# First stage of a two-layer decoder trunk: weights by quarters, and part of a modulation product as four column strips

## The chip, the cores and the metric

One core of a Trainium2 chip runs the whole program. The metric is the device time of one execution in microseconds (us). It is compared between the kernel before and the changed kernel; the median of three runs stands for the kernel before.

## What is computed

Two layers over `x` (1 x 512 x 1024, float32). Only the first mixer's beginning matters here:

```python
c_act = jax.nn.silu(c)
for l in range(DEPTH):
    mod = c_act @ ada_w[l] + ada_b[l]
    sh_m, sc_m, g_m, sh_f, sc_f, g_f = jnp.split(mod, N_MOD, axis=-1)
    h = modulate(rms_norm(x, norm_mix_g[l]), sh_m, sc_m)
    # layer 0: short_conv_mixer
    u = h @ w_in
    b_g, c_g, xv = jnp.split(u, 3, axis=-1)
    ...
```

`modulate` is `h * (1 + scale) + shift`. The first stage of the kernel is therefore: normalise x, compute the 2 x 1024 values `sh_m` and `sc_m` of layer 0 from a 1024 x 2048 piece of `ada_w`, form h, and multiply it with the first 512 columns of the `c_g` third of `sc_w_in`. All later stages (rest of the convolution mixer, MLP, attention, second MLP) are the same in both kernels.

## The kernel before, in words

Everything is kept transposed: a tile of h is 128 features by 512 tokens, and there are 8 of them (index j or k). Each float32 matrix product is made of three faster ones, with every operand split in a high part (rounded copy, on ACT) and a low part (what the rounding left, a subtraction on DVE): high by high, high by low, low by high (`products`, L589 to L592). A block is 128 output features: 8 tiles by three products into one bank of 512 columns. Four blocks form a group with banks 0 to 3 and weight slots 0 to 3.

The order of each engine is written out by hand, and the engines meet at counting semaphores. In the first stage:

- SP issues the loads in one order (L361 to L380): the four row tiles of x, then for each quarter q of the features 8 pieces of `ada_w` (`ada_quarter`, 256 KB each, into one of two buffers `ada_first`), with two weight blocks (`load_block`, 512 KB, rows of 512 bytes) behind each of quarters 0 and 1, and a fifth block (`early_raw`) behind quarter 3. A piece of quarter q waits until the same piece of quarter q-2 was used. Other rows and the next loads follow in the same queue.
- Modulation of a quarter: DVE multiplies pieces by the matching value of `c_act` and adds them up in `ada_acc` (`quarter_steps`, L1619): five pieces of quarter 0 and seven of each other. PE takes the remaining pieces (`quarter_direct`, L712) as products with one column each into bank 6, and adds the sum over the partitions of `ada_acc` (`quarter_sum`, L724). DVE adds the bias and makes the gain (`quarter_gain`, L1632).
- h tiles: ACT squares the rows of x (`token_square`, with the small Exp for silu behind the first of four, L1156 to L1160) and scales two of them, DVE the other two, into `x_unit`; PE transposes two tiles of a quarter into banks 4 and 5 (`unit_pair`, L700); ACT makes `tc` or `ta` and the high part (`first_tile`, L1169), DVE the low part (`first_low`, L1641).
- PE also transposes x itself for the residual stream (`x_turn`, L733; ACT copies it out, `x_tile`), and multiplies (`open_block`, L745). A block there waits for its whole weight block and its split. L754 to L788 write the order out.

Behind the stage PE transposes a few more rows (L791) and goes on with blocks 4 to 7 (L792 to L795), block 4 from its own early copy.

Of the kernel before, what the change touches and what calls it, by code (L numbers as in the profile page):

```python
# [54 lines left out]
ADA_STEPS = [(0, 1, 2, 3, 4)] + 3 * [tuple(range(KT - 1))]  # L55
ADA_DIRECT = [tuple(k for k in range(KT) if k not in steps) for steps in ADA_STEPS]
STEP_NO = {(q, k): n for n, (q, k) in enumerate((q, k) for q in range(QUARTERS) for k in ADA_STEPS[q])}
DIRECT_NO = {(q, k): n for n, (q, k) in enumerate((q, k) for q in range(QUARTERS) for k in ADA_DIRECT[q])}

# [35 lines left out]
def yoco_trunk(nc, x_in, c_in, ada_w, ada_b, norm_mix_g, norm_mlp_g, sc_w_in, sc_conv, sc_w_out,  # L95
# [23 lines left out]
    def stacked(offset, specs):  # L119
        made = []  # L120
        for name, shape, dt in specs:
# [31 lines left out]
    early_lo, = stacked(region_kv + size([P, KT, T + CONV - 1], F32) + size([P, NMOD * D], F32)  # L153
                        + size([P, TT, D], F32), [("early_lo", [P, KT, P], F32R)])
# [10 lines left out]
    raw, = stacked(region_w, [("raw", [P, GROUP, KT, P], F32)])  # L165
    rms = new("rms", [P, T], F32)
# [4 lines left out]
    early_hi, = stacked(region_qk + size([P, 2, T], F32), [("early_hi", [P, KT, P], F32R)])  # L171
# [3 lines left out]
    early_raw, = stacked(region_tb, [("early_raw", [P, KT, P], F32)])  # L175
# [3 lines left out]
    tv = new("tv", [P, T], F32)  # L179
# [40 lines left out]
    with ExitStack() as ctx:  # L220
# [23 lines left out]
        ada_direct = sem("ada_direct")  # L244
# [104 lines left out]
        def _(sp):  # L349
# [14 lines left out]
            def ada_quarter(q):  # L364

                for k in range(KT):
                    if (q - 2, k) in STEP_NO:
                        sp.wait_ge(ada_stepped, STEP_NO[q - 2, k] + 1)
                    elif q >= 2:
                        sp.wait_ge(ada_direct, DIRECT_NO[q - 2, k] + 1)  # L370
# [60 lines left out]
            for s in range(1, GROUP):  # L431
                sp.wait_ge(pe_done, s + 1)
# [153 lines left out]
        def _(pe):  # L586
# [16 lines left out]
            def dense(g, jj, hi, lo, ready=None, between=None, weights=None):  # L603
# [9 lines left out]
                elif weights:  # L613
                    last = part_of(b, 0, out, hi, lo, range(KT), ready, weights=weights)
# [85 lines left out]
            def unit_pair(q):  # L700

                for i in range(2):
                    j = 2 * q + i
                    if q:
                        pe.wait_ge(hs_ok, j - 1)
# [6 lines left out]
            def quarter_direct(q):  # L712
# [3 lines left out]
                for k in ADA_DIRECT[q]:  # L716
                    pe.wait_ge(ada_in[q % 2][k], 16 * (q // 2 + 1))
                    for n in range(4):
                        one = mm(bank[6][:, n:n + 1], ada_first[:, q % 2, k, n // 2, n % 2 * P:(n % 2 + 1) * P],
                                 c_act[:, k:k + 1], start=(k == ADA_DIRECT[q][0] and n == 0), stop=False,  # L720
                                 skip_group_check=True)
                    one.then_inc(ada_direct, 1)

            def quarter_sum(q):  # L724

                pe.wait_ge(ada_stepped, STEP_NO[q, ADA_STEPS[q][-1]] + 1)
                for n in range(4):
                    c = n // 2 * KT + 2 * q + n % 2
                    one = mm(bank[6][:, n:n + 1], ada_acc[:, c * P:(c + 1) * P], ones[:, 0:1], start=False,
# [15 lines left out]
            def open_block(b, tiles):  # L745

                last = part_of(b, b, bank[b], h_hi, h_lo, tiles, lambda k: pe.wait_ge(h_ok, H_MIX0 + k + 1))
                if tiles[-1] == KT - 1:
                    last.then_inc(pe_done, 1)
# [1292 lines left out]
```

## Time and profile before

| what | value |
|---|---|
| median of 3 runs | 1212.68 us (1211.74 to 1213.3) |
| the profiled execution | 1214.36 us |
| its span in the profile | 1211.7 us |
| granted TensorE clock, mean | 0.992 of full |
| PE busy | 1186.0 us, 98% of the span |
| DVE, ACT busy | 767.4 us (63%), 502.2 us (41%) |
| chain that ended last | PE 85%, DVE 7%, ACT 3%, issue 2% |

The span lies between the first and the last instruction; the execution's own time has 2.7 us around it. Busy time of PE says that something was in the array, not that it ran at its peak: the end of a matmul is modelled, and the clock can be granted at half. The chain is followed back from the last instruction to what released each step.

### The profile page before, as it was taken

To read this page: it belongs to the slowest core of one execution; us is meant where nothing else is said; L and a number is where in the kernel's file an instruction comes from. 1 tells how busy PE (TensorE), PEld (TensorE's weight loads), DVE (VectorE), ACT (ScalarE), POOL (GpSimd) and SP (SyncE) were. 2 spreads that over 40 slices of the span, in tenths; PEclk is the share of its full clock that TensorE was granted. 3 is DMA by queue.
4 is the path that set the end of the run, shared out by engine and by line. 5 is a ranking of instruction groups with operands and counts; after the bars stand their busy time and mean duration, and the time that the engine had idled before them with its cause. 6 is when DMAs were issued, how large, how long until landed. Compare 5 with 4: busy or idle time off the path is not lost.

```text
span 1211.7 us, 17089 instructions
## 1 busy us (share of the span) xinstructions
PE 1186.0 (98%) x5891; PEld 1000.2 (83%) x5891; DVE 767.4 (63%) x1117; ACT 502.2 (41%) x818; POOL 24.8 (2%) x37
## 2 busy tenths in 40 slices
PE   6999999999999999999999999999999999999998
PEld 5788888888888888888968888888888888888886
DVE  5557788876565575565888889886843443443441
ACT  5422332542331232332677777864631332331421
POOL 2000000000000000002020000000000000000000
PEclk7899999999999999999999999999999999999999
DMA  9487564466666665332345554451333333323333
GB/s 318 154 247 226 186 207 141 140 209 208 179 187 199 197 197 167 104 88 72 87 105 141 134 128 105 122 140 29 95 104 89 102 100 91 104 87 104 92 100 87
DMA packets 231697, 168.75 MB, mean 139 GB/s; under 512 B 5620, under 2 KB 214684, under 8 KB 231644
## 3 DMA queue, kind: packets, MB, share of 16 engines
q1 hardware_dynamic: 231452, 167.92, 47.8%
q8 instruction: 33, 0.54, 0.2%
q14 instruction: 20, 0.16, 0.0%
q0 software_dynamic: 32, 0.07, 0.0%
q10 hardware_dynamic: 160, 0.06, 0.0%
HBM read 153.24 MB, written 2.10 MB: 128 GB/s over the span
## 4 chain that ended last, share of the span: by engine, by line
PE 85%; DVE 7%; ACT 3%; issue 2%; DVEq 0%; ACTq 0%
PE bank L590 26%; PE bank L592 26%; PE bank L591 26%; PE bank L937 2%; PE bank L919 1%; PE bank L909 1%; PE bank L910 1%; DVE ta L1536 1%; DVE w_lo L1496 1%; DVE tc L1536 1%; ACT w_hi L1078 1%; PE bank L690 1%; DVE ada_acc L1719 0%; DVE h_lo L1545 0%; DVE h_lo L1543 0%
## 5 line engine op out<-in xcount | busy, mean ns | idle before, releaser
L590 PE MATMUL bank<-h_hi,w_hi 128*128 128x512 f32 (+1 forms) x888 | 338.3, 381 | 4.2 <-DVE w_lo L1496 1.7
L591 PE MATMUL bank<-h_lo,w_hi 128*128 128x512 f32 (+1 forms) x888 | 333.9, 376 | 0.0
L592 PE MATMUL bank<-h_hi,w_lo 128*128 128x512 f32 (+1 forms) x888 | 333.7, 376 | 0.0
L1078 ACT ACTIVATE w_hi<-raw 128x1024 fp32r<-128x1024 f32 x187 | 196.6, 1055 | 267.6 <-DMA raw<-in_mlp_w 221.2
L590 PE MATMUL bank<-g_hi,w_hi 128*128 128x512 f32 (+1 forms) x688 | 260.4, 379 | 0.0
L1496 DVE TENSOR_TENSOR w_lo<-raw,w_hi 128x1024 fp32r<-128x1024 f32 x187 | 227.9, 1221 | 47.7 <-ACT w_hi L1078 45.0
L592 PE MATMUL bank<-g_hi,w_lo 128*128 128x512 f32 (+1 forms) x688 | 257.8, 375 | 0.0
L591 PE MATMUL bank<-g_lo,w_hi 128*128 128x512 f32 (+1 forms) x688 | 257.6, 374 | 0.0
L590 PEld LDWEIGHTS bank<-h_hi,w_hi 128*128 128x128 f32 x888 | 168.2, 189 | 37.6 <-issue 6.8
L592 PEld LDWEIGHTS bank<-h_hi,w_lo 128*128 128x128 f32 x888 | 168.3, 190 | 30.1
L591 PEld LDWEIGHTS bank<-h_lo,w_hi 128*128 128x128 f32 x888 | 168.4, 190 | 29.4 <-issue 0.5
L592 PEld LDWEIGHTS bank<-g_hi,w_lo 128*128 128x128 f32 x688 | 129.5, 188 | 23.4
L591 PEld LDWEIGHTS bank<-g_lo,w_hi 128*128 128x128 f32 x688 | 129.6, 188 | 23.2 <-issue 0.5
L590 PEld LDWEIGHTS bank<-g_hi,w_hi 128*128 128x128 f32 x688 | 129.6, 188 | 22.9 <-issue 0.5
L1764 DVE SCALAR_TENSOR_TENSOR x<-bank,mod,x 128x512 f32 (+1 forms) x63 | 47.2, 750 | 141.1 <-PE bank L592 139.7
L1816 DVE TENSOR_TENSOR tb<-ta 128x512 f32<-128x512 f32 x64 | 44.3, 692 | 128.5 <-ACT ta L1276 128.5
L1276 ACT ACTIVATE ta<-bank 128x512 f32<-128x512 f32 x64 | 38.2, 597 | 197.7 <-PE bank L592 197.7
L1719 DVE SCALAR_TENSOR_TENSOR ada_acc<-ada_raw,c_act,ada_acc 128x1024 f32 (+1 forms) x80 | 102.2, 1277 | 2.3 <-DMA ada_raw<-in_ada_w 1.7
L1820 DVE TENSOR_TENSOR g_lo<-tb,g_hi 128x512 f32 (+1 forms) x64 | 44.3, 693 | 15.0 <-ACT g_hi L1278 12.5
L1278 ACT ACTIVATE g_hi<-ta 128x512 f32 x64 | 40.5, 633 | 8.1
L1381 ACT ACTIVATE probs<-bank,neg_max 128x512 f32<-128x512 f32 (+1 forms) x64 | 33.0, 526 | 26.2 <-DVE neg_max L1915 25.3
L1099 ACT ACTIVATE tb<-x 128x512 f32<-128x512 f32 x15 | 9.5, 632 | 55.4 <-DVE x L1764 49.7
(208 smaller groups left out, 1041.0 us busy)
## 6 DMA issues: line engine op xcount, KB each, us to landing
raw<-in_mlp_w SPq DMA_DIRECT2D x128, 512.0 KB, 4.1
ada_raw<-in_ada_w SPq DMA_DIRECT2D x40, 1024.0 KB, 5.7
raw<-in_sc_w_in SPq DMA_DIRECT2D x23, 512.0 KB, 5.9
ada_first<-in_ada_w SPq DMA_DIRECT2D x32, 256.0 KB, 7.1
raw<-in_w_kv SPq DMA_DIRECT2D x16, 512.0 KB, 4.0
raw<-in_sc_w_out SPq DMA_DIRECT2D x8, 512.0 KB, 4.4
raw<-in_q_w SPq DMA_DIRECT2D x8, 512.0 KB, 4.8
keys<-qk SPq DMA_DIRECT2D x16, 256.0 KB, 3.1
```

Source lines behind the costliest of these rows:

```text
L590: mm(out[:, cols], weights_hi, hi[:, k, cols], start=(k == 0), stop=False)
L591: mm(out[:, cols], weights_hi, lo[:, k, cols], start=False, stop=False)
L592: return mm(out[:, cols], weights_lo, hi[:, k, cols], start=False, stop=(k == KT - 1))
L1078: go(w_hi[:, jj, :, :], raw[:, jj, :, :], ACT.Copy).then_inc(hi_ok, 1)
L1276: go(ta[:, jj % 2, :], bank[jj][:], ACT.Relu).then_inc(bank_free, 1)
L1278: go(tile3(g_hi, j), ta[:, jj % 2, :], ACT.Square).then_inc(g_hi_ok, 1)
L1381: go(probs[:, P_OFF[qt]:P_OFF[qt] + n], bank[at_bank][:, c0:c0 + n], ACT.Exp, bias=neg_max[:, s:s + 1], accum_out=p_sum[:, s:s + 1]).then_ ...
L1496: tt(w_lo[:, jj, :, :], raw[:, jj, :, :], w_hi[:, jj, :, :], ALU.subtract).then_inc(lo_ok, 1)
L1719: stt(out=acc, in0=ada_raw[:, s, half * D:(half + 1) * D], scalar=col(c_act, k), in1=acc, op0=ALU.mult, op1=ALU.add).then_inc(ada_used, 1)
L1764: stt(out=tile3(x, j), in0=bank[jj][:], scalar=mcol(layer, part, j), in1=tile3(x, j), op0=ALU.mult, op1=ALU.add).then_inc(bank_free, 1)
L1816: tt(tb[:, s, :], ta[:, s, :], ta[:, s, :], ALU.mult).then_inc(g_a, 1)
L1820: tt(tile3(g_lo, j), tb[:, s, :], tile3(g_hi, j), ALU.subtract).then_inc(g_ok, 1)
```

## The change

The four column blocks of the first group are no longer loaded and split one by one. Their weights come as four quarters of rows (tiles 2q and 2q+1 for all 512 columns, 512 KB, rows of 2 KB), one behind each quarter of `ada_w`, and each quarter is split by one ACT and one DVE instruction of 1024 columns. PE takes the products tile by tile for all four blocks. Of each quarter's 8 pieces DVE steps the first four. PE takes the other four as float32 products of 512 columns: the stationary operand `c_wide[:, k, :]` is 32 columns wide (column 0 is `c_act`, the rest zero), and the output of strip i is partitions 32i to 32i+31 of bank 6. DVE then adds bank 6 to `ada_acc` (`quarter_add`). The odd h tile of each pair is scaled and shifted by DVE, no longer by ACT. The fifth block has no copy of its own: it is loaded into slot 0 once tiles 0 and 1 are used. ACT makes the small Exp behind all four squares.

```diff
@@ SP
             for q in range(QUARTERS):
                 ada_quarter(q)
-                if q < 2:
-                    load_block(2 * q, c_g(2 * q))
-                    load_block(2 * q + 1, c_g(2 * q + 1))
-            sp.wait_ge(hi_ok, 1)
-            sp.dma_start(early_raw[:], c_g(GROUP)).then_inc(raw_in[0], 16)
+                sp.dma_start(first_raw[:, 2 * q:2 * q + 2, :],
+                             sc_w_in[0].rearrange("(k p) n -> p k n", p=P)[:, 2 * q:2 * q + 2, D:D + GROUP * P]
+                             ).then_inc(raw_in[q], 16)
+            sp.wait_ge(first_used, 1)
+            load_block(0, c_g(GROUP))
...
@@ PE
-            def quarter_direct(q):
+            def quarter_strips(q):
 
                 if q:
                     pe.wait_ge(ada_red, q)
-                for k in ADA_DIRECT[q]:
+                for i in range(STRIPS):
+                    k = STRIPS + i
                     pe.wait_ge(ada_in[q % 2][k], 16 * (q // 2 + 1))
-                    for n in range(4):
-                        one = mm(bank[6][:, n:n + 1], ada_first[:, q % 2, k, n // 2, n % 2 * P:(n % 2 + 1) * P],
-                                 c_act[:, k:k + 1], start=(k == ADA_DIRECT[q][0] and n == 0), stop=False,
-                                 skip_group_check=True)
-                    one.then_inc(ada_direct, 1)
+                    mm(bank[6][32 * i:32 * i + 32, :], c_wide[:, k, :], ada_first[:, q % 2, k, :, :], start=True, stop=True,
+                       skip_group_check=True).then_inc(ada_strip, 1)
...
+            def first_products(k, blocks=range(GROUP)):
+
+                pe.wait_ge(lo_ok, k // 2 + 1)
+                pe.wait_ge(h_ok, H_MIX0 + k + 1)
+                for b in blocks:
+                    if k == 0:
+                        pe.wait_ge(x_ok, b + 1)
+                    w_cols = slice(b * P, (b + 1) * P)
+                    last = products(bank[b], first_hi[:, k, w_cols], first_lo[:, k, w_cols], h_hi, h_lo, k)
...
+            unit_pair(0)
+            pe.wait_ge(c_ok, 2)
+            quarter_strips(0)
+            x_turn(4)
             quarter_sum(0)
+            unit_pair(1)
+            quarter_strips(1)
+            first_products(0, range(0, 2))
+            quarter_sum(1)
+            first_products(0, range(2, GROUP))
+            first_products(1)
+            unit_pair(2)
+            quarter_strips(2)
...
@@ ACT
-            token_square(0)
+            for t in range(TT):
+                token_square(t)
             act.wait_ge(cols_ok, 1)
             go(c_tmp[:], cols[:, R_C:R_C + KT], ACT.Exp, scale=-1.0).then_inc(silu_e, 1)
-            for t in range(1, TT):
-                token_square(t)
...
@@ DVE
+            def quarter_add(q):
...
+                dve.wait_ge(ada_stepped, (q + 1) * STRIPS)
+                dve.wait_ge(ada_strip, (q + 1) * STRIPS)
+                tt(acc, bank[6][:].rearrange("p (a c) -> p a c", a=2), acc, ALU.add).then_inc(ada_added, 1)
+
+            def odd_tile(q):
...
+                ts(hs_slot(j, ALL), bank[5][:], gains[:, 0, j:j + 1], mcol(0, 0, j), ALU.mult,
+                   ALU.add).then_inc(odd_ok, 1)
```

Where instructions move. On PE, from the first transposes of x to the first products; names are output<-inputs, `ada_first` holds the pieces of `ada_w`, `x_unit` the normalised rows. Before:

```order
L742 MATMUL bank<-ident,x_rows 128x128 x20
L719 MATMUL bank<-c_act,ada_first 128x1 x12
L709 MATMUL bank<-ident,x_unit 128x128 x8
L729 MATMUL bank<-ones,ada_acc 128x1 x4
L742 MATMUL bank<-ident,x_rows 128x128 x4
L590 MATMUL bank<-h_hi,w_hi 128x512
```

and with the change:

```order
L741 MATMUL bank<-ident,x_rows 128x128 x16
L710 MATMUL bank<-ident,x_unit 128x128 x8
L720 MATMUL bank<-ada_first,c_wide 32x512 x4
L741 MATMUL bank<-ident,x_rows 128x128 x4
L728 MATMUL bank<-ones,ada_acc 128x1 x4
L710 MATMUL bank<-ident,x_unit 128x128 x8
L720 MATMUL bank<-ada_first,c_wide 32x512 x4
L592 MATMUL bank<-h_hi,first_hi 128x512
```

The second pair of transposes and the second quarter's strips now stand ahead of the first product; they stood behind it.

On DVE, quarter 0's sums and its gain, up to the first low part of h (`w_lo`, `first_lo` are the weight's low part). Before:

```order
L1671 TENSOR_SCALAR x_unit<-x_rows,tok 128x1024
L1629 SCALAR_TENSOR_TENSOR ada_acc<-ada_first,c_act,ada_acc 128x2x256 [waits ada_stepped,ada_in02]
L1629 SCALAR_TENSOR_TENSOR ada_acc<-ada_first,c_act,ada_acc 128x2x256 [waits ada_stepped,ada_in03]
L1629 SCALAR_TENSOR_TENSOR ada_acc<-ada_first,c_act,ada_acc 128x2x256 [waits ada_stepped,ada_in04]
L1496 TENSOR_TENSOR w_lo<-raw,w_hi 128x1024 [waits hi_ok]
L1636 TENSOR_TENSOR mod<-bank,ada_bias 128x2x2 [waits ada_turned]
L1615 SCALAR_TENSOR_TENSOR gains<-mod,cols 128x2 [waits ada_red]
```

and with the change:

```order
L1626 SCALAR_TENSOR_TENSOR ada_acc<-ada_first,c_act,ada_acc 128x2x256 [waits ada_stepped,ada_in03]
L1634 TENSOR_TENSOR ada_acc<-bank,ada_acc 128x2x256 [waits ada_strip,ada_stepped]
L1648 TENSOR_TENSOR first_lo<-first_raw,first_hi 128x1024 [waits hi_ok]
L1655 TENSOR_TENSOR mod<-bank,ada_bias 128x2x2 [waits ada_turned]
L1612 SCALAR_TENSOR_TENSOR gains<-mod,cols 128x2 [waits ada_red]
L1642 TENSOR_SCALAR tc<-bank,gains,mod 128x512 [waits unit_turned,mod_ok]
```

An addition that waits for all four strips stands ahead of the split and the gain, and one more h tile behind them.

## Rows read from the trace of the kernel before

**Rows 1.** By stretch: length; busy PE, PEld, DVE, ACT, POOL; granted clock, DMA, GB/s
```profile
0.00:22.50 22.50, 11.34 (x66) 10.61 (x66) 9.99 (x23) 14.02 (x24) 6.53 (x17) 0.90 1.00 317
22.50:62.60 40.10, 38.81 (x177) 32.70 (x178) 23.50 (x36) 15.79 (x23) 1.82 (x1) 0.80 0.63 188
62.60:110.00 47.40, 47.40 (x210) 38.92 (x209) 29.18 (x31) 13.40 (x15) 0.00 (x0) 1.00 0.81 247
```

**Rows 2.** Timeline: PE's first product, its idle time, and the stage's end
```profile
22.56 0.76 PE L590 MATMUL bank<-h_hi,w_hi 128*128 128x512 f32 x1 [1.04 <-DVE h_lo L1543]
...
40.15 1.05 PE L729 MATMUL bank<-ones,ada_acc 128*128 128x1 f32 x8 [1.22 <-DVE ada_acc L1629]
...
62.57 0.23 PE L791 MATMUL bank<-ident,rows_a 74*128 74x74 f32 x1
```

**Rows 3.** Chain that ended last: start, length, what; PE's pieces of the stage
```profile
42.48 0.43 PE bank L591
...
47.04 0.44 PE bank L742 x4
...
51.62 0.87 PE bank L709 x8
52.49 0.79 PE bank L719 x8
53.28 0.89 PE bank L729 x8
...
55.20 0.23 PE bank L591
```

**Rows 4.** Busy time by stretch again: granted clock where it is half, and before it rises
```profile
18.00:34.90 16.90, 14.57 (x53) 12.40 (x53) 13.36 (x22) 10.31 (x17) 0.00 (x0) 0.50 1.12 336
...
41.90:45.00 3.10, 3.10 (x9) 2.45 (x8) 2.33 (x4) 2.51 (x4) 0.00 (x0) 0.50 0.02 6
...
30.20:34.90 4.70, 4.70 (x14) 3.82 (x15) 3.60 (x8) 3.92 (x6) 0.00 (x0) 0.50 1.10 348
```

**Rows 5.** Groups of instructions up to 63 us: busy us, mean ns of one
```profile
L1629 DVE SCALAR_TENSOR_TENSOR ada_acc<-ada_first,c_act,ada_acc 128x512 f32<-128x512 f32 x22 | 16.5, 749 | 2.1 <-DVE ada_acc L1629 0.5 <-DMA ada_first<-in_ada_w 0.5
...
L1496 DVE TENSOR_TENSOR w_lo<-raw,w_hi 128x1024 fp32r<-128x1024 f32 x4 | 4.9, 1225 | 1.8 <-ACT w_hi L1078 1.8
...
L1078 ACT ACTIVATE w_hi<-raw 128x1024 fp32r<-128x1024 f32 x4 | 4.2, 1048 | 1.6 <-DMA raw<-in_sc_w_in 1.6
...
L1175 ACT ACTIVATE tc<-bank,mod,gains 128x512 f32<-128x512 f32 x4 | 3.1, 778 | 5.6 <-issue 5.6
...
L1543 DVE TENSOR_TENSOR h_lo<-tc,h_hi 128x512 fp32r<-128x512 f32 x4 | 2.8, 692 | 1.6 <-ACT h_hi L1178 1.6
```

**Rows 6.** Timeline of SP and ACT in the front, and issue to landing of x's loads
```profile
0.75 1.84 SPq L362 DMA_DIRECT2D x_rows<-in_x  x4
...
8.29 0.21 ACT L1158 ACTIVATE c_tmp<-cols 128x8 f32<-128x8 f32 x1 [2.58 <-DVE cols L1650]
...
13.07 2.19 ACT L1167 ACTIVATE x_unit<-x_rows,tok 128x1024 f32<-128x1024 f32 x2 [0.83 <-DVE tok L1667]
...
DMA to landing us min/median/max: 3.8/5.3/6.8
```

**Rows 7.** Rates of transfer (columns as in rows 1), and a wait for quarter 2's first piece
```profile
15.00:16.00 1.00, 1.00 (x11) 1.00 (x11) 0.89 (x2) 0.26 (x1) 0.00 (x0) 1.00 1.20 290
...
21.00:22.00 1.00, 0.52 (x3) 0.12 (x1) 0.28 (x1) 0.97 (x3) 0.00 (x0) 0.50 1.10 348
...
29.04 0.49 DVE L1626 TENSOR_SCALAR ada_acc<-ada_first,c_act 128x512 f32<-128x512 f32 x1 [0.60 <-DMA ada_first<-in_ada_w]
```

**Rows 8.** Float32 products of 256 columns (min/median/max ns), and split ones of 256 columns
```profile
L631 PE MATMUL bank<-ssum,ones x12: 377/380/484, 213.6 to 853.3; 128*128 128x256 f32 x12
...
848.90 0.28 PE L590 MATMUL bank<-o_hi,out_hi 128*128 128x256 f32 x1
849.02 0.28 PE L591 MATMUL bank<-o_lo,out_hi 128*128 128x256 f32 x1
```

More of the change, by code:

```diff
@@ L52 @@
 X_BANK = [0, 1, 2, 3, 7, 7, 7, 7]
[L55 to L58, printed above, removed]
+STRIPS = 4
 KVQ_ORDER = [("k", 0), ("v", 0), ("k", 1), ("q", 0), ("q", 1), ("v", 1)]
@@ L601, in part_of, with dense @@
                 return last
-            def dense(g, jj, hi, lo, ready=None, between=None, weights=None):
+            def dense(g, jj, hi, lo, ready=None, between=None):
                 if not isinstance(g, int) or g > 0:
@@ L612, in dense @@
                     last = part_of(b, s, out, hi, lo, range(6, KT), ready)
-                elif weights:
-                    last = part_of(b, 0, out, hi, lo, range(KT), ready, weights=weights)
                 else:
@@ L743, in x_turn @@
                 v.then_inc(x_turned, 1)
[L745 to L749, printed above, removed]
+            def first_products(k, blocks=range(GROUP)):
[6 more added lines that the diff above has]
+                    last = products(bank[b], first_hi[:, k, w_cols], first_lo[:, k, w_cols], h_hi, h_lo, k)
+                    if k == KT - 1:
+                        last.then_inc(pe_done, 1)
+                if b == GROUP - 1 and k % 2 and k < KT - 1:
+                    last.then_inc(first_used, 1)
@@ L780, in _ @@
-            quarter_direct(3)
-            quarter_sum(3)
-            open_block(2, Q[2])
-            open_block(3, Q[2])
-            for tile in Q[3]:
-                for b in range(2):
-                    open_block(b, range(tile, tile + 1))
-            open_block(2, Q[3])
-            open_block(3, Q[3])
+            unit_pair(1)
[4 more added lines that the diff above has]
+            first_products(1)
@@ new lines, in _ @@
+            unit_pair(2)
+            quarter_strips(2)
+            first_products(2, range(0, 2))
+            quarter_sum(2)
+            first_products(2, range(2, GROUP))
+            first_products(3)
+            unit_pair(3)
+            quarter_strips(3)
+            first_products(4, range(0, 2))
+            quarter_sum(3)
+            first_products(4, range(2, GROUP))
+            x_turn(5)
+            first_products(5)
+            x_turn(6)
+            first_products(6)
+            x_turn(7)
@@ L789, in _ @@
+            first_products(7)
             pe.wait_ge(rows_more, 16 * 8)
@@ L791, in _ @@
             turn(bank[7][:, 0:ROWS], rows_a[:], ident[0:ROWS, 0:ROWS]).then_inc(cols_pe, 1)
-            dense(1, 0, h_hi, h_lo, weights=(early_hi[:].rearrange("p (s k) c -> p s k c", s=1),
-                                             early_lo[:].rearrange("p (s k) c -> p s k c", s=1)))
-            for jj in range(1, GROUP):
+            for jj in range(GROUP):
                 dense(1, jj, h_hi, h_lo)
@@ L1183, in x_tile @@
                 go(x[:, j, :], bank[X_BANK[j]][:], ACT.Copy).then_inc(x_ok, 1)
[L1185 to L1195 removed]
+            for j in range(4):
+                x_tile(j)
+            split_first(0)
+            first_pair(0)
+            x_tile(4)
+            split_first(1)
+            first_pair(1)
+            split_first(2)
+            first_pair(2)
+            split_first(3)
             x_tile(5)
[L1197 to L1199 removed]
+            first_pair(3)
             x_tile(6)
[L1201 to L1203 removed]
+            split(1, 0)
             x_tile(7)
[L1205 to L1207 removed]
             act.wait_ge(unit_rest_ok, TT - 2)
@@ L1617, in gain, with quarter_steps @@
                 dve.wait_ge(mod_ok, count)
-            def quarter_steps(q, first, last):
+            def quarter_steps(q, first=0, last=STRIPS):
                 acc = ada_acc[:, 0:2 * D].rearrange("p (a q c) -> p a q c", a=2, q=QUARTERS)[:, :, q, :]
-                for k in ADA_STEPS[q][first:last]:
+                for k in range(first, last):
                     dve.wait_ge(ada_in[q % 2][k], 16 * (q // 2 + 1))
```

150 lines of the change are left out of this document (70 added, 80 removed).

## The prediction

> **What bounds the kernel.** I read the busy time by stretch first. From 62.6 us on PE is busy 47.40 of 47.40 us at full clock [rows 1], so whatever the first stage gains or loses is carried to the end unchanged. Only the end of that stage matters: the transpose at 62.57 us that closes it [rows 2]. In the front, up to 22.5 us, PE is half idle and waits for data and gains; from the first product at 22.56 us it is busy 38.81 of 40.10 us, but at a mean clock of 0.80 [rows 1, 2].
>
> Those 40.0 us can be taken apart with the pieces of the chain at full clock [rows 3]: 96 products by 0.228 us are 21.9; three pairs of h tiles transposed, by 0.87, are 2.6; three times the direct products of one piece, by 0.79, 2.4; three sums, by 0.89, 2.7; two transposes of x, by 0.44, 0.9. One wait of 1.2 us for DVE's last sum [rows 2] makes 31.7. The rest is clock: it is at half (1.2 GHz) from 18.0 to 34.9 us and from 41.9 to 45.0 us [rows 4], where a product takes 0.43 instead of 0.23 us [rows 3]. Of this 12.4 and 3.1 us lie behind the first product; half of it, 7.8 us, is lost. That explains 39.5 of 40.0 us; I keep the 0.5 us as what such a sum misses.
>
> **The change, part by part.**
>
> *Front.* ACT sat idle for 2.58 us before the small Exp, with three row tiles of x still to be squared behind it [rows 6]. x's fourth tile, the last of four issues from 0.75 to 2.59 us, so issued at about 2.2 us, and 6.8 us under way at the longest [rows 6], lands at 9.0. Without the wait its square ends near 10.3 instead of 11.6 us, so that the last scaled rows are ready at about 14.1 instead of 15.26 us (13.07 + 2.19) [rows 6]: 1.2 us earlier. PE's first four transposes of x and the Exp itself are hidden in front of that.
>
> *Loads.* Pieces of `ada_w` land every 0.75 us (256 KB at 348 GB/s), column blocks at 290 GB/s [rows 7]. Quarter 2's first piece landed at 29.04 us [rows 7]. Backwards from there, less its 0.75, four column blocks by 1.81 and quarter 1's eight pieces by 0.75, quarter 0's last piece landed at 15.1 us. It still does, and then 512 KB (1.5 us at 348 GB/s) instead of 1 MB (3.6 us) lie ahead of quarter 1: its last piece lands at 22.6 us, quarter 2's at 30.1, quarter 3's at 37.7. SP issues some 7 us ahead of the landing, and its new waits (for DVE's steps, for the strips of the quarter before last) are met before that. I cost the loads at nothing; the cover is PE's queue, which reaches quarters 2 and 3 at 35 and 44 us. Block 4's load now stands behind quarter 3 and the first two tiles' products, at about 34 us; it is wanted at 58 us. The rows and later loads queued behind it on SP are not needed before that either.
>
> *DVE and ACT.* DVE steps 16 pieces instead of 26: minus 10 by 0.75 us; plus four additions and four odd tiles, which I take at the 0.69 us of another pass over 512 columns [rows 5]; an addition reads a PSUM bank, so it can't be cheaper. The splits are 1.05 us on ACT and 1.23 us on DVE [rows 5], four as before plus the fifth. A quarter costs DVE 4 steps 2.7, addition 0.7, gain 0.4, odd tile 0.7, split 1.2 and two low parts 1.4: 7.1 us. PE needs 9.3 us for one (below), so I cost DVE at nothing behind the first gain; the wait of 1.2 us goes.
>
> *Strips.* They take the place of the direct products, four per quarter. The trace has no strip. A full float32 product of 256 columns shows two records of 0.38 us, where a split product of 256 columns shows one of 0.28 and its successor starts 0.12 us later [rows 8]; so each float32 record holds the array for 0.12 + 0.10 = 0.22 us, and a product of 512 columns takes two records by 0.43: 0.855 us. Four strips thus cost between 0.86 us (all at once) and 3.42 us (one behind the other). The nearest row is the full product's, two records in order on the same columns of the array. I take what follows when records are kept in order but those of different column strips may overlap: the second record of a strip runs beside the first of the next, five times 0.43, 2.14 us a quarter.
>
> The Trainium skill speaks on both sides of this. "TensorE: Matmul & The Clock Gate" (Part 3) says that products in different column groups run concurrently, with a measured 2.38 times for three column strips, and a span of one product plus some 4 ns per further strip; by that the strips would be the 0.86 us, and the sum 56.2. The same section says that weight loads overlap with running products only where the row group differs, which would put these strips, all on the same rows, one behind the other: the 3.42 us. This trace shows weight loads under products of the same rows (32.70 us of loads within 40.10 us in which PE is hardly idle [rows 1]), so it does not bear that rule out for full arrays; strips no row shows.
>
> *Chain to the start of the dense part.* Rows ready 14.1; pair transposed 15.0; strips 17.2; addition 17.9; split on DVE to 19.1; meanwhile sum to 18.9; gain 19.6; ACT's even tile (0.78 [rows 5]) 20.4. There PE takes the second pair, and from there on it always has work.
>
> *From there.* 96 products 21.9; three pairs 2.6; three quarters of strips 6.4; three sums 2.7; three transposes of x 1.3: 34.9 us. Clock: the two rises of before came 4.7 and 3.8 us after dense work had begun (30.2 to 34.9, and 41.2, behind the sum, to 45.0) [rows 2, 4]. Quarter 1's strips begin at about 22.3 us and end at 26.6 at half clock. If float32 strips count as dense the rise comes near 26.6, if not near 31; I take 28.5, so half speed from 20.4 to 28.5 loses 4.05 us. The fall at 41.9 had behind it 4 us of small products, transposes and a wait; that stretch is gone. With the 0.5 us: 20.4 + 34.9 + 4.05 + 0.5 = **59.9 us** against 62.57, minus 2.7 us.
>
> The profiled execution stands 1.7 us above the median (1214.36 against 1212.68). I put the difference on the median: **1210.0 us**. The bound below and above which a measurement of this kernel can tell a change from none is about 0.2%, 2.4 us: below 1210.3, above 1215.1.
>
> **Rivals.**
>
> A. *Strips all at once* (0.86 us). The quarter's addition ends at 16.6, but the split waits for its high part (16.6 + 1.05) and the even tile is out at 20.1; then 31.1 us of work, 0.6 of wait for quarter 1's last piece, 3.9 lost to the clock, 0.5: 56.2, which is 6.4 us less: 1206.3. For it: outputs lie on separate partitions. Against: two records per product, in order.
>
> B. *Strips one behind the other* (3.42 us), the slower side. Place: PE's queue, between a pair's transposes and the six products. The even tile comes at 21.7; 38.8 us of work, 4.05, 0.5: 65.0, or 2.5 us more: 1215.2. Each microsecond per quarter costs four, so this rival decides from 2.8 us per quarter on. For it: the only float32 rows. Then the change does not do what its strips are for, though weights, sums and clock still gain.
>
> C. *The clock stays at half longer.* Forecast as above, but the rise waits until 35 us, as it did before [rows 4], or a second fall comes: half of 6.5 us more, 63.1, 0.6 us slower: 1213.3. The six products between strips and sum speak against it.
>
> **How the numbers follow.** Forecast 50%, A 17%, B 25%, C 8%. The forecast's own range, with the clock's rise between 26.6 and 31 us and 1 us for the front, is 1208.2 to 1212.3; just over half of it is under 1210.3. Faster: 28 of the 50 and A's 17, and 2 of C: 47%. Within 0.2%: 22 of the 50, 6 of B (its centre is on the bound, but a late rise is more likely than an early one there), 5 of C: 33%. Slower: 19 of B, 1 of C: 20%. The range reaches from A, 1206.0, to B with a late rise, 1216.0.
>
> **What would show it.** The stage's closing transpose at 59 to 61 us. Records of strips: starts 0.43 us apart at full clock with strips overlapping, against all four within 0.9 us (A) or eight by 0.43 (B). The second pair at 20 to 21 us; no wait of PE for DVE from there on; one spell of half clock, ending at 27 to 31 us; PE gapless behind the stage. It would be wrong if PE waited for additions or low parts in every quarter, or if loads of the last quarters landed behind 45 us.

## The result, and the profile after

| | before | changed |
|---|---|---|
| median of the runs compared | 1212.99 us (4 runs) | 1205.43 us (4 runs, 1204.52 to 1205.57) |
| ratio | | 0.9925, 95% interval 0.9908 to 0.9941 |
| span in the profile | 1211.7 us | 1203.5 us |
| closing transpose of the stage | 62.57 us [rows 2] | 54.38 us |

The change is faster by 7.6 us, where 2.7 were forecast and 1206.0 was the lower end of the range. The closing transpose moved by 8.2 us and the span by 8.2: all of it lies in the first stage. The second run of the same kernel (below) closed at 54.18.

Busy time by stretch of the changed kernel (columns as in rows 1): the front, from the first product to the closing transpose, 47.4 us behind it, and the spell at half clock:

```profile
0.00:24.00 24.00, 12.95 (x62) 7.77 (x62) 12.78 (x28) 14.51 (x24) 6.53 (x17) 0.93 0.99 330
24.00:54.40 30.40, 30.40 (x166) 24.01 (x166) 18.76 (x31) 12.88 (x20) 1.82 (x1) 1.00 0.87 278
54.40:101.80 47.40, 47.32 (x210) 38.93 (x209) 29.34 (x31) 13.13 (x16) 0.00 (x0) 1.00 0.69 210
20.80:23.80 3.00, 3.00 (x9) 0.55 (x8) 2.90 (x5) 0.73 (x3) 0.00 (x0) 0.50 1.08 365
```

From the first product on PE is busy without a gap and at full clock (products start 0.23 us apart): 30.4 us, where rows 1 have 40.1 us at 0.80. The first product itself comes later than before, at 24.0 instead of 22.56 us, because a pair and the strips of quarter 1 now stand ahead of it.

PE's timeline in the changed kernel, without its products with h (start, length, what, and the idle time before it with its releaser):

```profile
14.63 1.26 PE L720 MATMUL bank<-ada_first,c_wide 128*32 128x512 f32 x8
15.82 0.66 PE L741 MATMUL bank<-ident,x_rows 128*128 128x128 f32 x4
16.87 1.05 PE L728 MATMUL bank<-ones,ada_acc 128*128 128x1 f32 x8 [0.40 <-DVE ada_acc L1634]
19.75 1.24 PE L710 MATMUL bank<-ident,x_unit 128*128 128x128 f32 x8 [1.83 <-ACT tc L1178]
20.92 3.18 PE L720 MATMUL bank<-ada_first,c_wide 128*32 128x512 f32 x8
25.52 0.95 PE L728 MATMUL bank<-ones,ada_acc 128*128 128x1 f32 x8
30.55 1.03 PE L710 MATMUL bank<-ident,x_unit 128*128 128x128 f32 x8
31.52 1.06 PE L720 MATMUL bank<-ada_first,c_wide 128*32 128x512 f32 x8
...
40.01 1.06 PE L720 MATMUL bank<-ada_first,c_wide 128*32 128x512 f32 x8
...
54.38 0.23 PE L791 MATMUL bank<-ident,rows_a 74*128 74x74 f32 x1
```

A float32 product of 512 columns leaves two records in the trace. Four strips, eight records, take 1.06 us, and only 1.0 us passes until the next instruction starts. The strips' own records in quarter 2, by stretch (length; busy PE, PEld; clock, DMA, GB/s), show them side by side:

```profile
31.50:31.70 0.20, 0.18 (x4) 0.16 (x8) 1.00 1.08 348
31.70:31.90 0.20, 0.20 (x4) 0.00 (x0) 1.00 1.07 338
31.90:32.50 0.60, 0.60 (x8) 0.00 (x0) 1.00 1.11 352
```

Four records are under way before 31.9 us. I read them as one per strip, since records on the same columns start 0.43 us apart (e1 below). All eight weight loads lie within 0.16 us, and they go on while these products already run. From 31.9 us on the second records join.

No sum after the first waits for DVE. The strips of quarter 1 take 3.18 us: the timeline of their weight loads shows 0.93 us of waits for pieces, the last of which landed at 22.22 us, and the clock was at half.

```profile
21.49 0.18 PEld L720 LDWEIGHTS bank<-ada_first,c_wide 128*32 128x32 f32 x2 [0.38 <-DMA ada_first<-in_ada_w]
22.22 0.18 PEld L720 LDWEIGHTS bank<-ada_first,c_wide 128*32 128x32 f32 x2 [0.55 <-DMA ada_first<-in_ada_w]
```

The chain that ended last, at the front (start, length, piece). It runs through the first quarter of the weight, not through x:

```profile
8.34 7.82 DMA first_raw<-in_sc_w_in
16.16 0.02 issue
16.18 1.06 ACT first_hi L1169
17.25 0.02 issue
17.27 1.23 DVE first_lo L1648
...
18.60 0.17 DVE gains L1612
```

DVE's timeline around quarter 1's sum shows that DVE now waits for PE, for the strips and for the sum:

```profile
24.21 0.69 DVE L1634 TENSOR_TENSOR ada_acc<-bank,ada_acc 128x512 f32<-128x512 f32 x1 [0.40 <-PE bank L720]
26.50 0.16 DVE L1655 TENSOR_TENSOR mod<-bank,ada_bias 128x4 f32<-128x4 f32 x1 [1.60 <-PE bank L728]
```

### The profile page after: what moved, and what is told of

The parts are those of the page before. It is cut to its first block, busy times and chain, and to the rows that moved or that the text cites. A ratio compares the mean times of both kernels' runs of the same rounds, so it can differ in the third digit from the quotient of the medians.

```text
span 1203.5 us, 17044 instructions
## 1 busy us (share of the span) xinstructions
PE 1179.1 (98%) x5875; PEld 989.4 (82%) x5875; DVE 765.7 (64%) x1118; ACT 499.3 (41%) x814; POOL 24.8 (2%) x37
## 4 chain that ended last, share of the span: by engine, by line
PE 85%; DVE 7%; ACT 3%; issue 2%; DMA 1%; SPq 1%; DVEq 0%; ACTq 0%
PE bank L592 26%; PE bank L594 26%; PE bank L593 26%; PE bank L935 2%; PE bank L917 1%; PE bank L907 1%; PE bank L908 1%; DVE ta L1533 1%; DVE w_lo L1493 1%; DMA first_raw<-in_sc_w_in 1%; DVE x L1788 1%; DVE tc L1533 1%; ACT w_hi L1076 1%; PE bank L690 1%; DVE ada_acc L1743 1%
## 5 line engine op out<-in xcount | busy, mean ns | idle before, releaser
L592 PE MATMUL bank<-h_hi,w_hi 128*128 128x512 f32 (+1 forms) x864 | 326.8, 378 | 3.2 <-DVE w_lo L1493 1.7
L594 PE MATMUL bank<-h_hi,w_lo 128*128 128x512 f32 (+1 forms) x864 | 323.2, 374 | 0.0
L593 PE MATMUL bank<-h_lo,w_hi 128*128 128x512 f32 (+1 forms) x864 | 323.1, 374 | 0.0
L1076 ACT ACTIVATE w_hi<-raw 128x1024 fp32r<-128x1024 f32 x184 | 193.4, 1054 | 257.9 <-DMA raw<-in_mlp_w 220.7
L1493 DVE TENSOR_TENSOR w_lo<-raw,w_hi 128x1024 fp32r<-128x1024 f32 x184 | 224.4, 1222 | 47.5 <-ACT w_hi L1076 44.7
L592 PEld LDWEIGHTS bank<-h_hi,w_hi 128*128 128x128 f32 x864 | 162.8, 188 | 34.2 <-issue 5.1
L594 PEld LDWEIGHTS bank<-h_hi,w_lo 128*128 128x128 f32 x864 | 162.8, 188 | 28.9
L593 PEld LDWEIGHTS bank<-h_lo,w_hi 128*128 128x128 f32 x864 | 162.9, 189 | 28.3 <-issue 0.5
L592 PEld LDWEIGHTS bank<-g_hi,w_hi 128*128 128x128 f32 x688 | 129.7, 189 | 22.7 <-issue 0.5
L1378 ACT ACTIVATE probs<-bank,neg_max 128x512 f32<-128x512 f32 (+1 forms) x64 | 33.0, 526 | 26.2 <-DVE neg_max L1939 25.3
```

The lines of the kernel that those rows point to most:

```text
L592: mm(out[:, cols], weights_hi, hi[:, k, cols], start=(k == 0), stop=False)
L593: mm(out[:, cols], weights_hi, lo[:, k, cols], start=False, stop=False)
L594: return mm(out[:, cols], weights_lo, hi[:, k, cols], start=False, stop=(k == KT - 1))
L1076: go(w_hi[:, jj, :, :], raw[:, jj, :, :], ACT.Copy).then_inc(hi_ok, 1)
L1378: go(probs[:, P_OFF[qt]:P_OFF[qt] + n], bank[at_bank][:, c0:c0 + n], ACT.Exp, bias=neg_max[:, s:s + 1], accum_out=p_sum[:, s:s + 1]).then_ ...
L1493: tt(w_lo[:, jj, :, :], raw[:, jj, :, :], w_hi[:, jj, :, :], ALU.subtract).then_inc(lo_ok, 1)
```

## The experiments

Two theories stood at the start. Theory 1: the four strips run side by side in the array; they are cheap, and with them the work is short. Theory 2: strips are not cheap, and the gain is clock, or the weights' new order. The runs also separate the change into its halves. Where nothing else is said, an experiment is an edit of the changed kernel, and its median is compared with runs of the kernel before on the same chip. Timelines and closing transposes come from the one profiled execution. In some runs it stood above the median: by 2.1 us in e2, 1.3 in e4, 1.0 in e8, 3.0 in e11, and 1.7 in the kernel before.

### e1: all strips on the same columns

```diff
-                    mm(bank[6][32 * i:32 * i + 32, :], c_wide[:, k, :], ..., start=True, stop=True,
+                    mm(bank[6][0:32, :], c_wide[:, k, :], ..., start=(i == 0), stop=(i == STRIPS - 1),
```

DVE adds 32 partitions instead of 128. A column group is what one strip takes, 32 of the array's 128 columns. 

> All four strips of a quarter are put on the same 32 columns of the array and accumulate there; only those 32 partitions are added. Theory 1 (the changed kernel's strips are cheap, 1.0 us for four, because they sit in different column groups and run beside each other): here four take 4 x 0.855 = 3.4 us at full clock. That is 2.4 us more in quarters 2 and 3 each, 2 to 4 in quarter 1 and 1 to 2 in quarter 0: the stage's closing transpose near 63 us instead of 54.4, the run 1213 to 1215 us. Theory 2 (a product with a stationary operand of 32 columns streams faster wherever it sits): four still take about 1 us and the run stays at 1205 to 1206 us.

Measured: 1214.28 us, ratio 1.0003 (0.9992 to 1.0015); closing transpose at 62.17 us. PE's timeline of that run, one row of the four:

```profile
34.22 3.62 PE L720 MATMUL bank<-ada_first,c_wide 128*32 128x512 f32 x8
```

The next instruction starts 3.55 us later. The same eight records on four column groups took 1.0 us. That is 2.55 us each in quarters 2 and 3. The second pair stands at 22.20 us, 2.45 later than in the changed kernel, and quarter 1's strips add only 0.4 us, since in the changed kernel they waited for pieces and ran at half clock. Without the overlap the whole change is worth nothing, although this run shows full clock in every stretch from 15 to 63 us. Theory 1 is right about the strips.

### e2: one-column products for the same four pieces

The strips are replaced by 16 products with one column, as the kernel before made them for its one or three pieces, and the addition goes. 

> The same four pieces per quarter as 16 one-column products in place of the strips, no addition on DVE. By queue time alone (16 by 0.2 us = 3.2 us instead of 1.0) quarters 1 to 3 cost 2.2 us more each and quarter 0 about 1: 1212 to 1213 us. Theory 3 (what also shortened the spell at half clock, 3.4 us in the changed kernel against 15.5 us behind the first product before, is that PE streams wide products where it had one-column ones): the clock falls again here, as early as 18 us, and is half for 10 us or more, so 3 to 5 us on top: 1215 to 1218 us. If the clock had nothing to do with it, one spell of 3 to 4 us stays.

Measured: 1228.49 us, ratio 1.0115 (1.009 to 1.014); closing transpose at 79.65 us. PE's timeline shows one quarter at half and one at full clock, and the stretches from 16 to 42 us and 50 to 55 us show why the time is so far above what was expected:

```profile
27.41 6.83 PE L721 MATMUL bank<-c_act,ada_first 128*128 128x1 f32 x32
...
45.58 3.63 PE L721 MATMUL bank<-c_act,ada_first 128*128 128x1 f32 x32
```

```profile
16.00:26.00 10.00, 8.61 (x42) 8.55 (x42) 3.52 (x8) 2.85 (x5) 0.00 (x0) 0.50 1.10 353
26.00:38.00 12.00, 12.00 (x53) 11.42 (x51) 3.44 (x6) 2.17 (x4) 0.00 (x0) 0.50 0.83 267
...
50.00:55.00 5.00, 5.00 (x18) 4.23 (x17) 2.04 (x4) 1.63 (x3) 0.00 (x0) 0.50 0.00 2
```

PE is busy 12.00 of 12.00 us from 26 to 38 us, with one-column products, then with products of 512 columns and a sum, and still has half clock. One-column products cost 3.6 us a quarter at full clock, and the clock was at half behind each lot of them: until 42 us behind the first two, and from 49.6 to 56.3 and 63.4 to 69.8 us behind the others. Its Theory 3 named the right direction and less than half of the size.

### e3 and e9: the weights' half of the change alone

Both keep the weights by quarters, the order by tiles, the odd tile on DVE and the late Exp, but give DVE its old five and seven pieces. e3 takes PE's remaining pieces as one-column products, without an addition on DVE; e9 takes them as strips, with one:

```diff
-                for i in range(STRIPS):
-                    k = STRIPS + i
+                n0 = 5 if q == 0 else KT - 1
+                for k in range(n0, KT):
+                    i = k - n0
```

> Weights by quarters, tile-by-tile order, late Exp and odd tile on DVE as in the change, but the sums divided as before: DVE steps 5 pieces of quarter 0 and 7 of the others, PE takes 3 and 1 as one-column products, no addition. If the strips are what the change gains by, this comes back most of the way: DVE needs about 8.9 us a quarter against 8.3 on PE, so PE waits up to 1 us for each sum, and the clock falls as before: 1209 to 1212 us. If weights and order are what it gains by, it stays within 1 us of the changed kernel: 1205 to 1207 us.

Measured: 1214.49 us, ratio 1.0003 (0.9989 to 1.0017); closing transpose at 64.30 us. PE waited 0.59 and 1.55 us for DVE's sums of quarters 1 and 3, and products started 0.43 us apart until 37.75 us.

> The changed kernel, but DVE steps 5 pieces of quarter 0 and 7 of each other, as before, and PE takes the other 3 and 1 as column strips (not as one-column products, as in e3_old_split, which gave 1214.5 us). Theory 1 (the moved share counts: DVE's longer steps of 7 pieces make PE wait for the sums, and that wait lets the clock fall, whatever form PE's products have): 1212 to 1215 us, half clock again in quarter 1 or 2, waits of 0.6 and 1.5 us for DVE's sums. Theory 2 (the form counts: wide strips in place of the one-column products keep the clock, so that only the waits for the sums stay): 1208 to 1210 us, that is the changed kernel's 1205.4 plus 2.1 of waits and 0 to 2 of clock.

Measured: 1212.36 us, ratio 0.9993 (0.998 to 1.0006); closing transpose at 61.15 us. PE's sums there:

```profile
28.08 1.05 PE L729 MATMUL bank<-ones,ada_acc 128*128 128x1 f32 x8 [0.71 <-DVE ada_acc L1636]
...
38.62 1.05 PE L729 MATMUL bank<-ones,ada_acc 128*128 128x1 f32 x8 [1.83 <-DVE ada_acc L1636]
...
49.17 1.05 PE L729 MATMUL bank<-ones,ada_acc 128*128 128x1 f32 x8 [0.22 <-DVE ada_acc L1636]
```

and its single strip of quarter 2, with what follows it:

```profile
34.15 1.05 PE L721 MATMUL bank<-ada_first,c_wide 128*32 128x512 f32 x2
35.12 0.50 PE L592 MATMUL bank<-h_hi,first_hi 128*128 128x512 f32 x1
```

Theory 1 of e9 was the one that held. Between e3 and e9 the medians differ by 2.1 us, but they were taken on different chips; by their ratios it is 0.1%, about 1.2 us, with intervals that overlap, so what the form alone is worth here is not settled. The changed kernel run beside e9 (e12) is faster by 6.3 us, and between the two only the division of the pieces differs: DVE takes three steps fewer in each quarter but the first, and one fewer there. DVE's gains in e9 come at 29.37 and 39.91 us, 10.54 us apart, with one wait of 1.14 us (for the sum on PE) between them, so DVE's round, with its way over PE's sum, sets the pace. A wait of 1.83 us is followed by half clock again, 3.0 us long:

```profile
40.80:43.80 3.00, 3.00 (x8) 2.34 (x7) 3.00 (x6) 2.24 (x4) 0.00 (x0) 0.50 0.00 0
```

### e13: the strips' half alone

The kernel before, with `ADA_STEPS = 4 * [(0, 1, 2, 3)]`, the other four pieces as strips, and DVE's addition in each quarter; all else as before. 

> The kernel before with the strips alone: DVE steps four pieces a quarter, PE takes four as column strips, DVE adds the bank; weights stay by blocks of columns, with their loads, the early fifth block, the order of the products, the tiles on ACT and the early Exp as before. Theory 1 (DVE's round of seven steps, 10.5 to 11 us from gain to gain, set the pace before; strips shorten it by 1.6 us of passes and that is the gain): the next gains come 9 to 9.5 us apart, closing transpose at 57 to 59 us, 1207 to 1210 us. Theory 2 (the halves need each other: with 1 MB of weights ahead of quarter 1's pieces and the splits of two blocks in one quarter, DVE and loads still set the pace): 1211 to 1214 us.

Measured: 1213.97 us, ratio 1.0 (0.9985 to 1.0015); closing transpose at 63.16 us. So this half gains nothing either. PE's timeline:

```profile
20.51 1.11 PE L744 MATMUL bank<-ident,x_rows 128*128 128x128 f32 x4 [2.38 <-ACT x L1186]
22.65 0.76 PE L594 MATMUL bank<-h_hi,w_hi 128*128 128x512 f32 x1 [1.03 <-DVE h_lo L1546]
...
28.87 1.05 PE L731 MATMUL bank<-ones,ada_acc 128*128 128x1 f32 x8 [0.96 <-DVE ada_acc L1640]
...
39.70 1.05 PE L731 MATMUL bank<-ones,ada_acc 128*128 128x1 f32 x8 [0.96 <-DVE ada_acc L1640]
```

DVE is relieved, but the old order puts the sum directly behind the strips, so each of the last three quarters waits 0.96 us for the addition. Before the second pair PE has only six products to do. And products start 0.43 us apart in three spells, from 22.7 to 25.3, from 29.8 to 32.4 and from 53.9 to 56.9 us. The 9 to 9.5 us between gains of its Theory 1 were not met: they came at 19.39, 30.73 and 41.00 us, and before the second and the third of them DVE waited 2.14 and 1.56 us for the strips. So Theory 2 had the time right and the reason wrong: behind the first gain it is PE, with its waits and the slow clock, and not DVE or the loads, that sets the pace here.

### e10: useless wide products in the kernel before

Three float32 products of 512 columns among quarter 0's one-column products, nine split ones around the transposes of x ahead of the first product, five ahead of quarter 2's sum; they are extra work. 

> The kernel before, plus useless wide products that keep PE's array at work where it idled or ran one-column products: 3 float32 ones of 512 columns among quarter 0's direct products, 9 split ones around the transposes of x ahead of the first product, 5 ahead of quarter 2's sum. They put up to 1.5 us of work on PE's queue ahead of the first product. Theory 1 (of the stage's 62.57 us, 7.8 are clock, and the change won most of its gain by them): the closing transpose at 57 to 59 us, 1207 to 1210 us. Theory 2 (the gain is the strips' own short time and the work ordered by tiles, clock only follows): 1212 to 1215 us.

Measured: 1212.98 us, ratio 1.0008 (0.9992 to 1.0023); closing transpose at 61.23 us.

```profile
14.00:30.00 16.00, 13.43 (x83) 10.45 (x84) 11.89 (x19) 8.79 (x14) 0.00 (x0) 1.00 1.14 323
30.00:33.50 3.50, 3.50 (x14) 2.81 (x14) 2.65 (x6) 2.30 (x4) 0.00 (x0) 0.56 1.10 348
```

```profile
29.55 1.09 PE L735 MATMUL bank<-ones,ada_acc 128*128 128x1 f32 x8 [2.09 <-DVE ada_acc L1640]
```

The stretches show that the clock was held up to 30 us; behind PE's wait of 2.09 us it was half once more, for the six products from 30.51 to 33.21 us, and the later spell of the kernel before (41.9 to 45.0 us) did not come. The timeline shows what became of it: the first six products ran at full speed and PE stood 2.09 us at the next sum. The useless products themselves put the first gain at 21.02 us (19.36 before) and the first product at 23.59 us (22.56 before). In spite of this the gains of quarters 1 and 2 came where they did in the kernel before. DVE's timeline of e10, and of the kernel before:

```profile
30.88 0.16 DVE L1626 SCALAR_TENSOR_TENSOR gains<-mod,cols 128x2 f32<-128x2 f32 x1
...
41.70 0.16 DVE L1626 SCALAR_TENSOR_TENSOR gains<-mod,cols 128x2 f32<-128x2 f32 x1
```

```profile
30.66 0.16 DVE L1615 SCALAR_TENSOR_TENSOR gains<-mod,cols 128x2 f32<-128x2 f32 x1
...
41.46 0.16 DVE L1615 SCALAR_TENSOR_TENSOR gains<-mod,cols 128x2 f32<-128x2 f32 x1
```

Clock alone was worth nothing in the first three quarters, because there DVE's round with its seven steps, not PE, set the pace. The 1.3 us in the closing transpose came behind them, and the median does not show it.

### e4 and e11: the Exp

e4 puts the small Exp of the changed kernel back behind the first square; e11 moves it behind all four in the kernel before.

> The changed kernel with ACT's small Exp back behind the first square. My prediction had 1.2 us for this in the front. Rival: the first weight quarter's landing at 16.2 us and its split, which stand ahead of the gain on DVE, set the start, and 1.2 us earlier rows gain nothing. First: closing transpose 1.2 us later, run near 1206.6. Rival: 0 to 0.3 us, run near 1205.6.

Measured: 1206.97 us, ratio 0.9946; closing transpose at 57.35 us, 3.0 later than in the changed kernel, and the median 1.5 us above it. About 1.2 us is the start; the rest is a longer spell at half speed (products 0.43 us apart until 27.8 us).

> The kernel before with one edit: ACT makes the small Exp behind all four squares of x, as in the changed kernel. Theory 1 (the forecast's 1.2 us at the front reach the first gain and stay): 1.2 us less than the kernel before. Theory 2 (the first gain there waits on the weight's split, whose load lands near 16 us whatever the squares do): within 0.5 us of before. A move of the clock's spell could add up to 2 us to either side, and would show in the distance of the products' starts.

Measured: 1213.34 us, ratio 0.9995 (0.9981 to 1.001), so its Theory 2 held: in the median the late Exp had no effect that shows. The profiled execution (1216.3 us) closed at 65.37 us, 2.8 later than the kernel before, with the first product only at 26.13 us behind 24 one-column records that took 5.12 instead of 3.08 us. That is the move of the slow spell which the expectation allowed for; three of the ten runs are above 1216 us, the others between 1212.8 and 1214.1.

### e5, e6, e7, e8 and e14: the front of the changed kernel

e5 puts the first six products ahead of quarter 1's strips, and the other six of tile 0 ahead of that quarter's sum. 

> The changed kernel with the first six products put ahead of quarter 1's strips. In the changed kernel these strips take 3.1 us (20.9 to 24.0), of which PE waits for landing pieces and runs at half clock, while the low part of the first h tile is ready at 21.0. If the products fill that wait, the tile's other products start about 0.9 to 1.4 us earlier: closing transpose 53.0 to 53.5 us, run 1204.0 to 1204.5. If PE's queue is no bound there (the later gains are), 0.

Measured: 1206.2 us, closing at 55.28: none of the gain. The first three products ran 0.43 us apart, the gain of quarter 1 came 1.4 us later, and PE waited 0.58 us for the addition of quarter 2. This run's second pair already stood 0.8 us later than the changed kernel's (20.58 us), ahead of anything that the edit moved.

e6 adds eight useless split products between the first sum and the second pair. 

> The changed kernel with eight useless split products of 512 columns (first weight quarter by itself, into bank 0, overwritten later) in PE's idle 1.83 us between quarter 0's sum and the second pair of transposes. If the fall of the clock at 20.5 us follows from what PE did not do up to then, it does not come, and of the 1.7 us that half clock cost all but the wait for landing pieces come back: 0.7 to 1.7 us, 1203.8 to 1204.8. If the fall comes by itself, nothing or up to 0.3 us slower.

Measured: 1205.41 us, closing at 54.78. The fall of the clock at 20.5 us did not come:

```profile
21.40 1.04 PE L710 MATMUL bank<-ident,x_unit 128*128 128x128 f32 x8
22.37 1.32 PE L720 MATMUL bank<-ada_first,c_wide 128*32 128x512 f32 x8
23.62 0.50 PE L592 MATMUL bank<-h_hi,first_hi 128*128 128x512 f32 x1
```

But the 0.7 to 1.7 us did not come either: the first product stands 0.4 us earlier, and a wait of 0.55 us for quarter 1's addition takes that away and more.

e7 has six of those, the order of e5, and DVE's split behind the odd tile. 

> Both together, with six products of filler, and DVE's split of the first weight quarter put behind the odd tile (the chain of the changed kernel shows landing 16.2, split on ACT, split on DVE, gain 18.6). If each works by itself and they add up: gain 0.4 us, tile order 0.9, clock 1 us earlier, 1202.8 to 1203.5, closing transpose 51.5 to 52.5 us. If quarter 1's landing at about 22.4 us bounds all of them, no more than the better of the two alone.

Measured: 1206.07 us, closing at 55.37, with 1.02 us of wait ahead of the first product and 0.64 for quarter 2's addition. The three did not add up.

e8 makes the odd tile on ACT behind the even one. 

> The changed kernel with the odd h tiles made by ACT again, as before the change. DVE gets 0.8 us a quarter back, ACT pays it, and the second tile's high part comes 0.8 us later. PE starts the next quarter's transposes behind it; in quarters 2 and 3 it has products in front, so only quarter 0 can show it: 0 to 0.8 us slower, 1205.4 to 1206.2.

Measured: 1207.32 us, closing at 57.43; PE's wait for the first tiles is 2.74 us instead of 1.83. So the odd tile on DVE is worth up to 1.9 us (medians from different chips), more than expected; the longer half-clock spell of this run, to about 28 us, is in that.

e14 moves DVE's first split behind the odd tile, and nothing else. 

> The changed kernel with DVE's first weight split behind the first odd tile, so that the first gain doesn't wait for the weight to land (16.16 us) and be split. Theory 1 (quarter 1's last pieces and its strips gate the first product anyway): gain 1 us earlier, the second pair 1 us earlier, but the first product and the closing transpose within 0.3 us of the changed kernel's 54.2 to 54.4; 1205 to 1206 us. Theory 2 (the wait of 1.8 us is on the path): closing transpose at 53.4, 1204.5 us.

Measured: 1205.03 us (1204.42 to 1205.29), closing at 54.22, with the second pair at 19.75 us and the first product at 23.80. The gain came at 18.60 us, no earlier than in the changed kernel, because the first strips and sum stood 0.4 us later in this run; the wait ahead of the pair is 0.44 us shorter by that alone. So its Theory 1 was not put to a real test here. e6 is the better witness: its second pair stood at 21.40 us, 1.65 us later than in the changed kernel, and its first product at 23.62, 0.4 us earlier. What the first product waits for is the last piece of quarter 1 (22.22 us in the changed kernel) and the strip behind it, which takes 1.0 us at full clock and 1.8 at half (e9's single strips); the waits ahead of the pair are hidden in front of that. None of these variants is faster than the changed kernel by more than its own runs differ.

### e12: the changed kernel again

> The changed kernel itself, once more, beside e9 to e11 on the same chip: 1205 to 1206 us; the closing transpose at 54 to 55 us. If the half-clock spell ahead of or behind the second pair lies elsewhere than in the first profile (20.5 to 24.0 us), its place is chance from run to run, and up to 1 us between two variants is not to be read as an effect of their edits.

Measured: 1206.03 us (1205.06 to 1206.45), ratio 0.9939 (0.9919 to 0.9958), closing at 54.18. The two medians of the one kernel differ by 0.6 us; those of e5, e6, e7 and e14 lie inside or just beside that.

## Why the prediction was wrong

The direction and the place were right, the size was not. The forecast's sum was 20.4 + 34.9 + 4.05 + 0.5 = 59.9 us for the closing transpose. With what was measured it is 19.75 + 31.5 + 2.3 + 0.5 = 54.05, against 54.38 in the profile; 2.3 us is what the slow clock and the waits for pieces cost together. The step that failed is the price of the strips; the clock is the second.

- **Strips** ("I take what follows when records are kept in order but those of different column strips may overlap", 2.14 us a quarter) is the step that failed first. There is no such order between the strips: four records, read as one of each, run at once before the second ones start. Rival A's price, 0.86 us, was nearly right: 1.0 us measured. Three quarters by 1.14 us are 3.4 us of the 34.9. e9 gives the same from the other side: a single strip, two records, keeps PE for 0.97 us there (34.15 to 35.12), nearly as long as four do. Serial records (rival B, 3.42 us) are what e1 shows, 3.55 us, when the strips share their columns. The rows of before could not tell these apart, but the range of 0.86 to 3.42 us held the value, and I gave its best end a chance of 17 in 100.

The Trainium skill's "TensorE: Matmul & The Clock Gate" (Part 3) has products in different column groups run concurrently; the runs agree (1.0 us against 3.55 us). Its rule that a weight load overlaps with running products only where the row group differs spoke for rival B. Here all strips used all rows, and their loads still ran under products (eight loads within 0.16 us while four products were under way), so the measurement decides against it for these strips.

- **Clock** ("half speed from 20.4 to 28.5 loses 4.05 us"). The spell ended at about 24.0 us. The second pair and quarter 1's strips took 4.28 us (19.75 to 24.03), where 1.97 us are their length at full clock. Of the 2.3 us between, 0.93 are waits for pieces, which the sum had at nothing, and about 1.4 are clock and the overlap lost by the waits. So the term for the clock was 2.7 us too high, and clock and waits together 1.7. I had taken the time of the rise from the kernel before, where transposes, one-column products and waits lay in between. Behind wide strips it came sooner; why is not settled, since in other variants (e4, e8) the spell lasted until about 28 us with the same strips.
- **Front** (20.4 us). The second pair came at 19.75. The 1.2 us of the Exp are in this, but the gain at 18.60 waited for the weight's landing and split, not for x. And as e6 shows, what happens there is hidden ahead of the landing of quarter 1's last piece (forecast at 22.6 us, measured at 22.22). Rival A's 0.6 us of wait for it was 0.93.
- **DVE** ("costed at nothing behind the first gain") held in the changed kernel, with a smaller margin than claimed. I counted 7.1 us a quarter against PE's 9.3. Measured are 8.49 us for PE. DVE was busy 6.6 us of these, less than I counted, but I left out that it has to wait for the sum on PE before it can make the gain. With that its round would be some 8.3 us, an estimate from e9's 10.54 less three steps of 0.75. That fits with e5, e6 and e7, which met waits of 0.55 to 0.64 us for the addition as soon as something moved.
- **What bounds the kernel before** ("the rest is clock ... 7.8 us is lost"). The arithmetic was right and the reading wrong. e10 took away all but about 3 us of the 15.5 us at half clock, and got 1.3 us in the profile and nothing in the median: a PE at full clock waits for DVE. The slow clock had hidden DVE's round of seven steps, 10.8 us between two gains, and so the one wait of 1.2 us in rows 2 said too little. By this the three steps taken from DVE in a quarter (2.2 us, less 0.7 for the addition) were a condition of the gain, and e9, which gives them back, shows it.
- **Parts or whole.** Weights and order alone: 1212.4 to 1214.5 us. Strips alone: 1214.0. Both: 1205.4. What fits the timelines is that the strips free DVE, and that only the order by tiles gives PE six products while the addition runs: e13 waits 0.96 us at each of its last three sums, the changed kernel at none. No run changes this order alone, and the late Exp and the odd tile on DVE went with the weights' half throughout; with the whole change in place they are worth up to 1.5 and 1.9 us (e4, e8), so they are not what e13 lacks most. I had taken the parts' effects as a sum.

What stays open: what ends a spell at half clock. Its length differed between variants with the same instructions behind it.

## What to carry to other kernels

A slow clock and a slow partner engine hide each other: before pricing either, lay the other engine's round (here the distance between two gains) beside this one's work at full clock, and take the longer. Small float32 products with narrow stationary operands should go to different column groups of the array; here four cost what one costs. When two halves of a change each relieve a different bound, test both alone: here neither gained anything by itself.

## What the runs showed of the hardware that was not expected

- Eight float32 records of 512 columns took 3.55 us on one column group and 1.0 us on four; one strip alone took 0.97 us.
- PE can be "busy" throughout and yet have half clock: 12.00 of 12.00 us at 0.50 in e2, with one-column products at the start. Two of e2's four lots of 16 such products ran at full clock themselves, but half clock followed each of the four.
- Eight weight loads of 32 columns and all rows lay within 0.16 us, partly under running products of the same rows.
- The granted clock in the rows can miss a spell. In e4 the stretch from 14.6 to 18.6 us shows 1.00, while the timeline has seven transposes in 2.10 us and four strips in 1.94 us, about twice their length at full clock:

```profile
14.60:18.60 4.00, 3.88 (x16) 1.49 (x17) 2.64 (x4) 3.64 (x6) 0.00 (x0) 1.00 1.09 356
```

```profile
14.64 2.10 PE L710 MATMUL bank<-ident,x_unit 128*128 128x128 f32 x7 [0.19 <-DVE x_unit L1688]
16.67 1.94 PE L720 MATMUL bank<-ada_first,c_wide 128*32 128x512 f32 x8
```

So the distance between starts is the surer sign, and the "full clock in every stretch" of e1 rests on that too (its strips took 3.62 us in all four quarters). In e3, products stood 0.43 us apart until 37.75 us in stretches that show 1.00.
